# An RWKV-7 scan on one Trainium2 core: 128-row state products, a block-diagonal copy of the state, and three scaling steps moved from VectorE to GpSimd

## The reference, cut to what matters

```python
def step(s, inp):
    sa = einsum('bhvk,bhk->bhv', s, kk_t)
    s = s * w_t[:, :, None, :] - sa[..., None] * (kk_t * a_t)[:, :, None, :] + v_t[..., None] * k_t[:, :, None, :]
    return s, einsum('bhvk,bhk->bhv', s, inp[5])      # r_t; only latent tokens give an output
```

## Time and profile before

| | before |
|---|---|
| median of 3 runs | 2254.05 us (2246.99 to 2255.99) |
| the profiled execution's own time | 2254.09 us |
| span of its trace | 2252.2 us |
| TensorE, VectorE, ScalarE, GpSimd busy | 91%, 61%, 35%, 12% |
| granted TensorE clock, mean | 0.951 |
| the scan, between the barriers at its two ends | 972.6 to 1286.6 us |

### The profile page before, as it was taken

How to read it: one execution, slowest core, us unless ns; L and a number is a source line. 1 busy time by engine, 2 the same in 40 slices (tenths; PEclk the granted TensorE clock), 3 DMA queues, 4 the chain that set the end, 5 groups by cost and what they waited for, 6 DMA issues and landing times. The chain is left out here.

```text
span 2252.2 us, 38698 instructions
## 1 busy us (share of the span) xinstructions
PE 2045.4 (91%) x16787; PEld 1684.7 (75%) x16787; DVE 1363.5 (61%) x1287; ACT 789.7 (35%) x858; POOL 275.8 (12%) x135
## 2 busy tenths in 40 slices
PE   7679999999899989966666799989999999999997
PEld 3268888888589867656666688778888888888886
DVE  3465666665438447768877778466565656554444
ACT  1231111113162225524433365344443434333333
POOL 0242213124105214401000020000000000000000
PEclk9589999999899999988999999999999999999998
DMA  9978888886353378986444187545555555555552
GB/s 334 348 272 327 314 308 305 311 310 181 106 155 103 85 210 260 302 189 171 85 85 87 46 192 260 210 132 179 194 187 194 187 187 186 186 199 193 188 200 97
DMA packets 406151, 454.17 MB, mean 202 GB/s; under 512 B 107550, under 2 KB 356750, under 8 KB 388734
## 3 DMA queue, kind: packets, MB, share of 16 engines
q1 hardware_dynamic: 398400, 441.04, 61.3%
q10 hardware_dynamic: 7614, 11.10, 1.3%
HBM read 413.89 MB, written 38.22 MB: 201 GB/s over the span
## 5 line engine op out<-in xcount | busy, mean ns | idle before, releaser
L215 DVE TENSOR_TENSOR f_w_lo<-t_w_raw,f_w_hi 128x2048 fp32r<-128x2048 f32 x132 | 302.5, 2291 | 307.7 <-ACT f_w_hi L209 307.7
L270 PE MATMUL pf<-h,f_w_hi 128*128 128x512 f32 x1320 | 463.9, 395 | 0.0
L209 ACT ACTIVATE f_w_hi<-t_w_raw 128x2048 fp32r<-128x2048 f32 x132 | 253.4, 1920 | 446.3 <-PE pf L270 283.5
L269 PE MATMUL pf<-h,f_w_lo 128*128 128x256 f32 x1320 | 367.4, 278 | 0.3 <-DVE h L2586 0.3
L270 PEld LDWEIGHTS pf<-h,f_w_hi 128*128 128x128 f32 x1320 | 247.6, 188 | 54.3
L269 PEld LDWEIGHTS pf<-h,f_w_lo 128*128 128x128 f32 x1320 | 248.3, 188 | 4.6 <-DVE h L2586 0.6
L209 ACT ACTIVATE p_w_hi<-h_w_raw 128x2048 fp32r<-128x2048 f32 (+1 forms) x52 | 96.4, 1903 | 340.6 <-DVE stage L726 252.1
L261 PE MATMUL p_in<-h,p_w_lo 128*128 128x512 f32 (+1 forms) x512 | 199.3, 389 | 0.0
L259 PE MATMUL p_in<-h,p_w_hi 128*128 128x512 f32 (+1 forms) x512 | 199.3, 389 | 0.0
L260 PE MATMUL p_in<-h,p_w_hi 128*128 128x512 f32 (+1 forms) x512 | 199.2, 389 | 0.0
L2782 PE MATMUL d_out<-f_w_hi,hid 128*128 128x512 f32 x704 | 178.8, 394 | 6.1 <-DVE f_w_lo L215 6.1
(11 more groups left out here) (417 smaller groups left out, 3371.1 us busy)
## 6 DMA issues: line engine op xcount, KB each, us to landing
h_of_x<-in_ada_w SPq DMA_DIRECT2D x64, 1024.0 KB, 5.0
h_w_raw<-in_w_in SPq DMA_DIRECT2D x51, 1024.0 KB, 7.3
t_w_raw<-in_ffn_w_gate SPq DMA_DIRECT2D x44, 1024.0 KB, 5.1
t_w_raw<-in_ffn_w_up SPq DMA_DIRECT2D x44, 1024.0 KB, 5.1
t_w_raw<-in_ffn_w_down SPq DMA_DIRECT2D x44, 1024.0 KB, 4.9
h_w_raw<-in_ada_w SPq DMA_DIRECT2D x32, 1024.0 KB, 8.8
gate_w<-in_w_in SPq DMA_DIRECT2D x32, 1024.0 KB, 5.9
t_w_raw<-in_w_out SPq DMA_DIRECT2D x16, 1024.0 KB, 5.6
```

Source lines behind the costliest of these rows:

```text
L209: act.activation(self.hi[:, m % self.S, 0:w], self.raw[:, s, 0:w], ACT.Copy)\
L215: eng.tensor_tensor(self.lo[:, m % self.S, 0:w], self.raw[:, s, 0:w], b32(self.hi[:, m % self.S, 0:w]), ALU.subtract)\
L269: pe.matmul(hi, wl, x[:, 0, k, :], start=False, stop=False)
L270: return pe.matmul(both, wh, x[:, :, k, :], start=False, stop=last)
```

## The change

It touches the scan and, for the layout of the factors, the preparation.

- **The factors.** The two factors of a pair swap planes in every odd pair, and are loaded into a tile of their own, `s12[P, pair, 2, C]`. One DMA (`ldr`, 768 KB) becomes three (`ld` and two for `s12`, 256 KB each).
- **GpSimd** takes over `prepare1`, `prepare2` and `prepare3`, and does the split of the GLA output in rounds 8 and 10 (`ends` of the chunks 4 and 5).
- **Flips.** One transpose turns both factors of one pair, so `s21t[:, 2j+h]` holds the key in one half of the partitions and the other factor in the other. `vu` is laid out the same way: v in one half, u in the other. ScalarE writes it by two copies of 64 partitions each for v (`tokens`) and two for u (`u_step`), in place of one of 128 each.
- **State.** s2t by v and s1t by u become one product over 128 rows: 16 products (32 records) in place of 32 (64 records).
- **S.** A block-diagonal copy `Sx[P, pair, 2, C]` of S is written by ScalarE (`spread`, two copies of 64 partitions), and `rhs_sum` and `from_state` are each 8 products (16 records) over 128 rows in place of 16 (32 records).
- **Inverse.** Two products of the identity by 256 columns (4 records) put the identity into PSUM, TensorE waits for them on its own semaphore, and the 16 products add to it; ScalarE scales by half in place of VectorE. `own_part` and `inverse` come ahead of `prepare(ahead)` in the list.
- **Output.** TensorE waits on its own semaphore (`y_own`) between the two parts.

```diff
-                    sp.dma_start(ldr[d][:].rearrange("p a u t -> p (a u) t"), dir_d[d, :, :, at:at + C])\
+                    sp.dma_start(ld[d][:], dir_d[d, :, 0:U8, at:at + C]).then_inc(sm("in", d), 16)
+                    for x in range(2):
+                        sp.dma_start(s12[d][:, :, x, :], dir_d[d, :, U8 * (x + 1):U8 * (x + 2), at:at + C])\
...
+                go("spread", last)
                 go("scores1", now)
...
+                go("own_part", lev)
+                go("inverse", lev)
                 if not early:
                     go("prepare", ahead)
-                go("own_part", lev)
-                go("inverse", lev)
...
                 def tokens(c, d):
                     act.wait_ge(sm("vtr", d), c + 1)
-                    act.activation(quads(vt[d][:]), narrow(pb[d]), ACT.Copy).then_inc(sm("vt", d), 1)
+                    for x in range(2):
+                        act.activation(quads(vu[d][HEAD[x], x]), narrow(pb[d])[HEAD[x]], ACT.Copy).then_inc(sm("vt", d), 1)
...
+                def inverse(c, d):
+                    act.wait_ge(sm("k", d), c + 1)
+                    act.activation(quads(xt[d][:]), narrow(pa[d]), ACT.Copy, scale=0.5).then_inc(sm("inverse", d), 1)
+                def spread(c, d):
+                    act.wait_ge(sm("S", d), c + 1)
+                    for h in range(2):
+                        act.activation(Sx[d][HEAD[h], :, h, :], S[d][HEAD[h]], ACT.Copy).then_inc(sm("spread", d), 1)
...
+                def prepare1(c, d):
+                    pool.wait_ge(sm("es", d), c + 1)
+                    pool.wait_ge(sm("in_s", d), c * 32 + 32)
+                    pool.tensor_tensor(s12[d][:], s12[d][:], es[d][:].unsqueeze(2).broadcast_to([P, U8, 2, C]), ALU.mult).then_inc(sm("s12", d), 1)
+                def prepare2(c, d):
+                    if c:
+                        pool.wait_ge(sm("rhs", d), c)
+                    pool.tensor_tensor(q12[d][:, :, 0, :], kkv[d][:, 0], decays(d, 1), ALU.mult).then_inc(sm("q1", d), 1)
+                def prepare3(c, d):
+                    if not first_latent(c):
+                        pool.wait_ge(sm("y", d), c - 4)
+                    pool.tensor_tensor(q12[d][:, :, 1, :], rc[d][:], decays(d, 0), ALU.mult).then_inc(sm("q2", d), 1)
...
                 def inverse(c, d):
+                    for b in range(2):
+                        last = pe.matmul(pa[d][:, b * BANK:b * BANK + BANK // 2], eye[:],
+                                         eyes[:, 4 * b:4 * b + 4, :].rearrange("p u c -> p (u c)"), start=True, stop=False,
+                    last.then_inc(sm("ones", d), 1)
+                    pe.wait_ge(sm("ones", d), c + 1)
...
                 def rhs_sum(c, d):
-                    for j, h in UNITS:
-                        last = pe.matmul(by_token(pb[d], j, h), feat(q12[d][:, :, 0, :], j, h), feat(S[d], j, h), start=False, stop=True, skip_group_check=True)
+                    for j in range(U8):
+                        last = pe.matmul(in_flips(pb[d], j, 0, j % 2, 2), q12[d][:, j, 0, :], Sx[d][:, j].rearrange("p x c -> p (x c)"),
+                                         start=False, stop=True, skip_group_check=True)
...
                 def state(c, d):
-                    for four in FOURS:
-                        for j, h in four:
-                            pe.matmul(by_feature(pa[d], j, h, 1), flip(s2t[d], j, h), flip(vt[d], j, h), start=True, stop=False)
-                        for j, h in four:
-                            last = pe.matmul(by_feature(pa[d], j, h, 1), flip(s1t[d], j, h), tok(u[d], j, h), start=False, stop=True)
+                    for j in range(U8):
+                        for h in range(2):
+                            last = pe.matmul(by_feature(pa[d], j, h, 1), s21t[d][:, 2 * j + h, :], vu[d][:, j % 2, j // 2 * 2 + h, :],
+                                             start=True, stop=True)
```

More of the change, by code:

```diff
@@ L1423, in _ @@
                     own = eye[HEAD[h], HEAD[h]]
[L1424 to L1425 removed]
+                    for t in cross + first + [eyes]:
                         dve.tensor_copy(t[HEAD[h]], own.unsqueeze(1).broadcast_to([C, U8, C])).then_inc(sm("init", 0), 1)
@@ L1438, in prepare @@
                     dve.tensor_tensor_scan(out=flat(b[d])[:, rev], data0=keep[:],
-                                           data1=ldr[d][:, 0].rearrange("p u c -> p (u c)")[:, rev], initial=0.0,
+                                           data1=flat(ld[d])[:, rev], initial=0.0,
                                            op0=ALU.mult, op1=ALU.add).then_inc(sm("b", d), 1)
[L1442 to L1460, removed]
                 def turn(c, d, l, src):
@@ L1531, in output @@
                     dve.tensor_tensor(by_parity(yat), by_parity(yat), narrow(pb[d]), ALU.add).then_inc(sm("ysum", d), 1)
-                run(dict(prepare=prepare, prepare1=prepare1, prepare2=prepare2, prepare3=prepare3, stage=stage, scores1=scores1, scores2=scores2,
-                         close=close, open=open_, inverse=inverse, state=state, output=output))
+                run(dict(prepare=prepare, stage=stage, scores1=scores1, scores2=scores2,
+                         close=close, open=open_, state=state, output=output))
             @block.scalar
@@ L1592, in _ @@
+                def spread(c, d):
+                    if c == LAST:
+                        return
+                    act.wait_ge(sm("S", d), c + 1)
+                    for h in range(2):
+                        act.activation(Sx[d][HEAD[h], :, h, :], S[d][HEAD[h]], ACT.Copy).then_inc(sm("spread", d), 1)
                 run(dict(prepare=prepare, ends=ends, output=output,
-                         tokens=tokens, flips=flips, stage=stage, close=close, rhs=rhs_copy, u=u_step))
+                         tokens=tokens, flips=flips, stage=stage, close=close, rhs=rhs_copy, u=u_step,
+                         inverse=inverse, spread=spread))
@@ new lines, in ends @@
+                def ends(c, d):
+                    if (c, d) == (CTX // C, 0):
+                        pool.wait_ge(sm("gla_in", 0), 16)
+                        pool.tensor_copy(yb[:, 0], g[:]).then_inc(sm("gla_hi", 0), 1)
+                    if (c, d) == (CTX // C + 1, 0):
+                        pool.wait_ge(sm("gla_hi", 0), 1)
+                        pool.tensor_tensor(yb[:, 1], g[:], b32(yb[:, 0]), ALU.subtract).then_inc(sm("gla_lo", 0), 1)
+                run(dict(prepare1=prepare1, prepare2=prepare2, prepare3=prepare3, ends=ends))
@@ L1666, in turn_all, with turn_factors @@
                         last = pe.transpose(p[d][:, at:at + P], t[:, j:j + 2, :].rearrange("p u c -> p (u c)"), eye[:])
+                    return last
+                def turn_factors(p, pairs, d):
+                    for j in pairs:
+                        at = (j // 2 % 2) * BANK + (j % 2) * P
+                        last = pe.transpose(p[d][:, at:at + P], s12[d][:, j].rearrange("p x c -> p (x c)"), eye[:])
                     return last
@@ L1725, in u_step @@
                     for j, h in UNITS:
-                        last = pe.matmul(by_token(pa[d], j, h), tok(xt[d], j, h), tok(rhs[d], j, h), start=True, stop=True)
+                        last = pe.matmul(in_flips(pa[d], j, h, 1 - j % 2), tok(xt[d], j, h), flip(rhs[d], j, h), start=True, stop=True)
                     last.then_inc(sm("u", d), 1)
```

102 lines of the change are left out of this document (61 added, 41 removed).

## The result

The changed kernel takes **2285.85 us** (median of 4 runs, 2284.78 to 2289.58) against 2254.99 for the one before (4 runs, 2246.99 to 2255.99): a ratio of 1.0149 [1.0127, 1.0172], slower by 31 us. The forecast was 2262, the range ended at 2286.

A forecast was written before the change was run, and what follows sets the result against it. It took the scan as bound by TensorE and VectorE handing levels to and fro, neither full, plus TensorE's program waits. Seven context rounds +1.8, eight latent +5.2 and tail +1 gave +8.0 on 2254.1: 2262 us, range 2236 to 2286.

The forecast's parts named there:

- GpSimd and VectorE at once: Scan: GpSimd's scalings make VectorE's masks wait, 0.75 us a context half (level 1), 1.65 a latent half (level 4).
- The GLA split blocked a mask before and will again, in another round: nothing: Scan: GpSimd's split of the GLA output holds up a mask as before, in another round, at no added time.
- Fewer records: Scan: fewer TensorE records shorten program gaps, 1.4 us off a latent half and 0.3 off a context half.
- the walk: One scan round stepped through from its opening transpose, before and after: -0.2 us in a context half, +0.4 in a latent one.
- The start of the round: Opening to level 0: second v copy and identity put level 0's product at 3.4 us; transpose +1.15 context, +1.55 latent.
- Width of a product: Scan's 128-row products run in pairs: rhs, state and from_state 0.85 us each; from_state 1.7 if loading 128 columns sets it.
- records over 40 ns apart: Sign in rhs and state that 128-row products don't pair, making each 0.85 us longer.
- Changes between whole and divided array: TensorE's tiling changes in the scan: 0.2 us beside each new group between levels, 0.2 to 0.6 a half.
- The tail: Last two rounds, without scores: the longer start and the second copy of u show, +1 us.
- Unpaired products: Rival: 128-row products don't pair, or each change drains, 1.2 us a half, +19, 2281 us; chance 0.24.
- GpSimd waits: Rival: in the scan GpSimd waits instead of VectorE, the 18.5 us fall out, 2243.5 us; chance 0.20.
- Program supply: Rival: TensorE's program supply is the bound; 768 fewer records save 21 us, 2233 us; chance 0.14.

The follow-up runs named there:

- e4: Changed kernel with all three scalings back on VectorE, the GLA output's split still on GpSimd in rounds 8 and 10: 2261.66 us, 1.0029 of before.
- e1: Changed kernel with the split of the GLA output moved to the end of GpSimd's list: 2285.8 us.
- e9: Changed kernel with GpSimd's split of the GLA output put behind the last cross operation of the scan: 2282.86 us.
- e15: Changed kernel with the GLA split behind the scan's last cross operation and prepare1 in four GpSimd instructions: 2272.03 us.
- e10: Changed kernel with prepare1, the 1,024-element scaling, cut into four GpSimd instructions of 256 elements: 2281.19 us.
- e8: Changed kernel with the scalings on VectorE, the inverse as before and from_state in 64-row products from S: 2250.72 us, 0.9991 of before.
- e7: Changed kernel with the scalings on VectorE and the inverse as before, without the identity's products: 2247.92 us, 0.9985 of before.

## Why the prediction was wrong

It named the direction of GpSimd's cost and its mechanism, and missed the sum by 22 us against the profiled 2284.78. By its own steps, predicted and measured: context +1.8 and -0.1, latent +5.2 and +23.5, tail +1 and +6.6. Without GpSimd's 18.5 it had the change at -10.5 us; e4, which has no scaling on GpSimd, is at +9.8 by the profiled times (+6.7 by the medians). **So nearly all of the miss lies outside GpSimd's term.**

- **GpSimd and VectorE at once**: +18.5 predicted (7 x 0.75 + 8 x 1.65); e4's trace gives 20.9 us (2284.78 to 2263.85). The size held, in part by luck: 6.0 us of the hold-up are the split's, which stood at nothing. The place did not hold: one hit of 1.6 us in the context, where `es` came at +4.4 behind the inverse's copy, VectorE's mask went first and GpSimd paid, and about 2.4 a latent round, where 1.65 stood. The 1.65 was mis-added too: with the last transpose at 12.7 the mask was due at 13.45, 0.75 behind it as at level 1, and would have waited 2.05. The step counted one hit a round, the mask of level 4. The scaling of S was hit in four rounds and the decay scan in two, one of each by the split.
- **"The GLA split blocked a mask before and will again, in another round: nothing"**: wrong in its reason. Before it held a mask for 2.7 us; after, it held the decay scan and the scaling of S for 1.7 and 4.3. Moving it gave at most 3 us by itself (e1, e9) and 9 on top of the quarters (e15 against e10).
- **Fewer records**, -1.4 a latent round and -0.3 a context round, -13.3 in all, taken off a walk of +0.4 and -0.2: **the step that failed.** The gaps did shrink, by more than I said, from 45.1 us to 17.7 in e4 (39.2 to 9.5 without the ones that are waits), but e4's latent rounds are 20.39 us, before's 19.94. In latent rounds, without those waits, e4 has 2.6 us less of gaps a round, where -1.4 stood, and 3.0 us more of everything else, where the walk had +0.4. I took the credit off the one round shown, 20.92 us with a gap of 2.98, when the mean of the eight was 19.94; 20.92 + 0.4 - 1.4 is 19.9, near e4's 20.39, and no gain on 19.94. A gap and the chain beside it are not two terms that add: e8 against e7 shortens the one and lengthens the other. With the identity undone too, e7's latent rounds are 19.26. No run gives the records alone.
- **The start of the round**: level 0's product 3.4 us after the opening forecast, 3.54 measured in the context round (1089.23 to 1092.77) and 3.75 in the latent one, but A is 5.17 in the mean even of e4 (4.2 forecast), where the last flip starts 1.29 us after most openings (0.61 in the walk) and the clock in the mean is 0.95. The code's largest cost was rightly named; e7 against e4 prices it at 10 to 14 us, and no relief of VectorE made up for it.
- **Width of a product**: rhs and state do pair. The 16 loads of rhs take 0.85 us, as forecast, and the 32 products of state 1.15 where 0.85 was. The sign that I set, records over 40 ns apart, fits state (30 ns) and not rhs, whose forecast of 0.85 us for 16 is itself 53 ns apart (55 measured). from_state went past the upper bound that I had named and put aside: 2.00 us against 1.7 "if the loading of 128 columns sets it", and C is 3.15 in e4 where the walk had 2.4. That is +0.75 a latent round.
- **Changes between whole and divided array**: I put 0.2 each. In the round above level 0's group (1203.91) is followed by rhs's 128-row group 0.57 us later, and the same kind of group follows in one form after 0.52 (1203.39 to 1203.91); level 2 starts 1.93 us after the 2.00 us of from_state began. So at most 0.1, and of the drain that the Trainium skill (TensorEngine Tiling (Array Packing), Key Properties) gives for a change of mode these rows show nothing.
- **The tail**, +1: 6.6. It has no scores to hide work behind, so the identity (2.8, e7) and the wide from_state (2.1, e8) stand in its chain; the rest I put down to the second copies, which no run undoes. It is 27.3 us in e4, where no scaling runs on GpSimd.
- **Rivals.** Unpaired products (2281) lay nearest in time and were wrong in cause; only from_state behaved so. "GpSimd waits" was right for the context alone. Program supply falls as the one bound: gaps a third as long, and the kernel slower.

Of what the prediction listed as signs, the masks of 2.1 us beside the 1024-wide product and context rounds of 16.4 came; latent rounds were longer than the 20.5 to 22, and VectorE's sum fell by 22 us: in the scan by 25.4 (242.1 to 216.7), near the 45 less the 18 of hold-up that came in, and outside it grew by 3.7.

## What to carry to other kernels

Before an elementwise step is moved to GpSimd, list VectorE's operations with two SBUF inputs that lie on the chain and place them against the GpSimd instruction's whole length; a hit costs until that instruction ends, so cut it short or put it where VectorE goes first. Take a credit for a shorter wait only after checking, in the mean of the rounds and not in one of them, what else ends at that point. And judge an edit with its neighbours undone as well: the identity's 10 to 14 us showed as 4 while the scalings were on GpSimd.

## What the runs showed of the hardware that was not expected

- GpSimd's product of 512 elements took 1.2 to 2.1 us in the scan and not the 1.02 of the earlier trace rows; in e10 256 elements took 0.87, so four cost 3.5 where one of 1024 costs 2.6 in the mean.
- Sixteen products with 128 loaded columns and 64 streamed took 2.00 us, 125 ns each; sixteen of rhs, with 64 loaded and 128 streamed, took 1.09. Here the group with more loaded columns was the slower, though it streams half as many; its loads alone took 1.86 us against 0.85.
- The granted clock of the stretch E that holds the wait of 5.87 us was 0.55, and 14.6 us of redundant products brought the mean of all latent rounds from 0.89 to 0.97 at no cost in time.
